# State-space period of a hybrid decoder layer laid out anew: x turned by VectorE, decays a group ahead, taps spread, norm factor on GpSimd

## The reference, cut to what matters

```python
xbc = jax.nn.silu(causal_dwconv(xbc, ssm_conv_w, ssm_conv_b))      # 4 taps
xs, bm, cm = jnp.split(xbc, (D_INNER, D_INNER + SSM_GN), axis=-1)
# in ssd_chunked, with chunks of 128 tokens:
x = (xh * dt[..., None])
decay = jnp.exp(jnp.where(causal, a_cum[..., :, None] - a_cum[..., None, :], -jnp.inf))
cb = jnp.einsum('bclgn,bcsgn->bcgls', cc, bc)
y_diag = jnp.einsum('bcgls,bgrcls,bcsgrp->bclgrp', cb, decay, x)
...
y = y + d_skip[:, None] * xh
y = y * jax.nn.silu(z)
y = y * lax.rsqrt(jnp.mean(y * y, axis=-1, keepdims=True) + NORM_EPS)   # per group of 512
```

## Time and profile before

| | us |
|---|---|
| median of 3 runs | 1932.03 (1931.19 to 1932.3) |
| the profiled execution | 1931.42, of which the span in the trace is 1929.7 |
| TensorE busy | 1916.6 (99%) |
| VectorE busy | 1266.2 (66%) |
| ScalarE busy | 1083.3 (56%) |
| GpSimd busy | 38.3 (2%) |

### The profile page before, as it was taken

How to read it: one execution, slowest core, us unless ns; L and a number is a source line. 1 busy time by engine, 2 the same in 40 slices (tenths; PEclk the granted TensorE clock), 3 DMA queues, 4 the chain that set the end, 5 groups by cost and what they waited for, 6 DMA issues and landing times.

```text
span 1929.7 us, 28955 instructions
## 1 busy us (share of the span) xinstructions
PE 1916.6 (99%) x10258; PEld 1629.8 (84%) x10258; DVE 1266.2 (66%) x1534; ACT 1083.3 (56%) x1474; POOL 38.3 (2%) x79
## 2 busy tenths in 40 slices
PE   9999999999999999999999999999999999999998
PEld 7888888888888878888888888888888888888886
DVE  6777788777878874445444555767766667645444
ACT  6467766677657764444344445666666666534443
POOL 1000000000011100000000000000000000000000
PEclk9999999999999999999999999999999999999999
DMA  7666666656654446666666565666666666665554
GB/s 246 188 191 178 197 190 193 189 171 196 205 163 133 130 132 211 194 194 194 194 191 195 175 239 192 194 185 192 187 194 193 186 185 189 189 198 195 192 193 141
DMA packets 294839, 361.53 MB, mean 187 GB/s; under 512 B 13104, under 2 KB 217968, under 8 KB 293360
## 3 DMA queue, kind: packets, MB, share of 16 engines
q1 hardware_dynamic: 294768, 360.59, 61.0%
HBM read 358.38 MB, written 2.16 MB: 187 GB/s over the span
## 4 chain that ended last, share of the span: by engine, by line
PE 99%; issue 0%; DMA 0%; ACT 0%; DVE 0%; SPq 0%; POOLq 0%; POOL 0%; DVEq 0%; ACTq 0%
PE ps L1405 35%; PE ps L1407 18%; PE ps L1390 14%; PE ps L1391 13%; PE ps L1392 13%; PE ps L1598 1%; PE ps L1526 1%; PE ps L1539 1%; PE ps L1550 0%; PE ps L1599 0%; PE ps L1587 0%; PE ps L1442 0%; DMA raw<-w_in 0%; PE ps L1477 0%; PE ps L1732 0%
## 5 line engine op out<-in xcount | busy, mean ns | idle before, releaser
L870 DVE TENSOR_TENSOR lo<-raw,hi 128x1024 fp32r<-128x1024 f32 x656 | 801.3, 1227 | 518.7 <-ACT hi L449 511.7
L1405 PE MATMUL ps<-uHL,hi 128*128 128x512 f32 x2944 | 1035.5, 396 | 0.0
L449 ACT ACTIVATE hi<-raw 128x1024 fp32r<-128x1024 f32 x656 | 687.2, 1055 | 517.1 <-PE ps L1392 386.2
L1407 PE MATMUL ps<-uHL,lo 128*128 128x256 f32 x2944 | 823.9, 280 | 0.0
L1405 PEld LDWEIGHTS ps<-uHL,hi 128*128 128x128 f32 x2944 | 551.7, 187 | 130.7 <-issue 5.5
L1407 PEld LDWEIGHTS ps<-uHL,lo 128*128 128x128 f32 x2944 | 555.9, 189 | 0.0
L1392 PE MATMUL ps<-hi,aL 128*128 128x512 f32 x384 | 149.5, 389 | 0.0
L1392 PE MATMUL ps<-hi,hL 128*128 128x512 f32 x352 | 136.9, 389 | 0.0
L1391 PE MATMUL ps<-lo,hH 128*128 128x512 f32 x352 | 136.9, 389 | 0.0
L1390 PE MATMUL ps<-hi,hH 128*128 128x512 f32 x352 | 136.9, 389 | 0.0
L454 ACT ACTIVATE hb<-ps 128x512 f32<-128x512 f32 x92 | 54.7, 595 | 121.3 <-PE ps L1407 121.3
(11 more groups left out here) (195 smaller groups left out, 1657.2 us busy)
## 6 DMA issues: line engine op xcount, KB each, us to landing
raw<-w_in SPq DMA_DIRECT2D x265, 512.0 KB, 4.3
raw<-w_ffn_in SPq DMA_DIRECT2D x176, 512.0 KB, 3.7
raw<-w_ffn_out SPq DMA_DIRECT2D x88, 512.0 KB, 4.5
raw<-w_ssm_out SPq DMA_DIRECT2D x64, 512.0 KB, 4.4
raw<-w_attn_out SPq DMA_DIRECT2D x32, 512.0 KB, 4.3
raw<-w_o SPq DMA_DIRECT2D x32, 512.0 KB, 4.3
rows_b<-cum_rows SPq DMA_DIRECT2D x8, 1024.0 KB, 6.8
x_tok<-x SPq DMA_DIRECT2D x8, 256.0 KB, 6.0
```

What stands on the lines that cost most here:

```text
L449: act.activation(hi[:, s % SLOTS, :], raw[:, s % SLOTS, :], ACT.Copy).then_inc(hi_ready, 1)
L870: ve.tensor_tensor(lo[:, s % SLOTS, :], raw[:, s % SLOTS, :], hi[:, s % SLOTS, :].bitcast(F32), ALU.subtract).then_inc(lo_ready, 1)
L1405: pe.matmul(ps[:, pair + c, :], w_hi, uHL[:, kk].rearrange("p a n -> p (a n)"), start=kk == 0, stop=False)
L1407: last = pe.matmul(ps[:, pair + c, 0:SEQ], w_lo, uHL[:, kk, 0, :], start=False, stop=kk == k - 1)
```

## The change

What it does, engine by engine:

- **TensorE** no longer transposes x. `b_dot_c` keeps the two B·C products behind unit 2; `y_of` moves from unit 9 to 11, `mean_y` from 16 to unit 0 of the next period, `turn_root` from 0 to 4.
- **VectorE** transposes x itself in `x_turn`: blocks of 32x32, four instructions behind each of the units 3 to 6, each on 32 partitions and 256 elements, from `sv` to `xd`. The product with dt then works in place. The taps stand in units 9 and 10, 13 and 14, 17 to 19. The blocks stand behind 11 and 12, skip 15, gate 16, sum 19 (two additions for one reduction), mean 3, spread 4, scale 8. `scaled` gives way to `halves` alone.
- **GpSimd** multiplies by `rt` in place (`scaled_in`, five times a period), with the root between.
- **ScalarE** has `conv_start` behind 8, 12, 16, `silu_gate` behind 5, squares behind 18. The next group's `drops` stand behind 15, 16, 17, its first Exp behind 19, the second Exp and the crosses behind 0 and 1. The first group's (`first_decays`) are written apart: behind 0, 1 and 6.
- **SyncE** has `row_load` between units 7 and 8, for every group but the first.

The diff, cut to its core:

```diff
@@ sync
                 columns(U_G + 4, d, "in", g * GW + C_X, KD)
+                if g:
+                    sp.wait_ge(rows_used, g)
+                    row_load(g)
                 columns(U_G + 8, d, "in", g * GW + (C_X + W2), KD)
...
             for g in range(1, G):
                 group(g, g * G_UN)
-                sp.wait_ge(rows_used, g)
-                row_load(g)
                 group_end(g, g * G_UN)
@@ gpsimd
-            with po.Fori(0, G) as g:
-                y_root(g)
+            def scaled_in(t, odd, it, q, done):
+                po.wait_ge(pair_free[(A, B)[(5 * odd + q) % 2]], it * 5 + ((5 * odd + q) // 2 + J_G + 1))
+                po.tensor_tensor(t, t, rt[:, None, :].to_broadcast([P, 2, SEQ]), ALU.mult).then_inc(done, 1)
+            def conv_and_z(odd, it):
+                for q in range(3):
+                    scaled_in(cs[:], odd, it, q, cs_ready)
+                scaled_in(szb[:, 0:2, :], odd, it, 3, z_scaled)
...
+            with po.Fori(1, G // 2) as it:
+                for odd in range(2):
+                    scaled_in(szb[:, 2:4, :], 1 - odd, it + (odd - 1), 4, z_scaled)
+                    y_root(it * 2 + (odd - 2))
+                    conv_and_z(odd, it)
@@ scalar
+            def decay_side(k, u):
+                if u == 15:
+                    drops(k, 0, 0)
+                if u == 16:
+                    drops(k, 0, 1)
+                if u == 17:
+                    drops(k, 1, 0)
+                    drops(k, 1, 1)
+                if u == 19:
+                    decays(k, 0)
+            def decay_rest(k, u):
+                if u == 0:
+                    decays(k, 1)
+                    cross_decays(k, 0, 3)
+                if u == 1:
+                    cross_decays(k, 3, HG)
+                    rows_done(k)
+            def first_decays(u):
+                if u < 2:
+                    for half in range(2):
+                        drops(0, u, half, first=True)
+                if u == 6:
+                    for c in range(2):
+                        decays(0, c)
+                    cross_decays(0, 0, HG)
+                    rows_done(0)
@@ vector
+                    if u == 9:
+                        conv_taps(g * 6, bc_tiles, 0, 2)
+                    if u == 10:
+                        conv_taps(g * 6, bc_tiles, 2, 3)
+                    if u == 13:
+                        conv_taps(g * 6 + 2, low_tiles, 0, 2)
+                    if u == 14:
+                        conv_taps(g * 6 + 2, low_tiles, 2, 3)
+                    if u in (17, 18, 19):
+                        conv_taps(g * 6 + 4, high_tiles, u - 17, u - 16)
...
+            def x_turn(k, q):
+                ve.wait_ge(sv_ready, k + 1)
+                src = sv[q * B32:(q + 1) * B32, 0:4, :].rearrange("p i (c n) -> p i c n", c=TT)
+                for j in range(P // B32):
+                    dst = xd[j * B32:(j + 1) * B32, :, :].rearrange("p c (i n) -> p i c n", i=4)
+                    ve.transpose(dst[:, :, :, q * B32:(q + 1) * B32], src[:, :, :, j * B32:(j + 1) * B32])
...
-                ve.tensor_reduce(ysum[:, :, None], ysq[:].rearrange("p i n -> p n i"), op=ALU.add, axis=AX.X) \
-                    .then_inc(y_summed, 1)
+                ve.tensor_tensor(ysq[:, 0:2, :], ysq[:, 0:2, :], ysq[:, 2:4, :], ALU.add)
+                ve.drain()
+                ve.tensor_tensor(ysum[:], ysq[:, 0, :], ysq[:, 1, :], ALU.add).then_inc(y_summed, 1)
...
-            STEPS = dict(inputs=5, low=8, high=9, skip=12, gate=13, sum=17, mean=19)
+            STEPS = dict(turn=(3, 4, 5, 6), cb=7, inputs=7, low=11, high=12, skip=15, gate=16, sum=19, mean=None)
@@ tensor
-                pe.matmul(ps[:, M, 2 * P:3 * P], sv[:, 4, P:SEQ], sv[:, 5, P:SEQ], start=True, stop=True)
-                for c in range(TT):
-                    for i in range(4):
-                        last = pe.transpose(ps[:, M + 1 + c, i * P:(i + 1) * P], sv[:, i, c * P:(c + 1) * P], ident[:])
-                last.then_inc(x_turned, 1)
+                pe.matmul(ps[:, M, 2 * P:3 * P], sv[:, 4, P:SEQ], sv[:, 5, P:SEQ], start=True, stop=True) \
+                    .then_inc(bc_done, 1)
...
-            def ssd_after(k, u, older=True, at=(2, 9, 16)):
+            def ssd_after(k, u, older=True, at=(2, 11, None)):
                 if u == 0 and older:
+                    mean_y(k - 1)
+                if u == 4 and older:
                     turn_root(k - 1)
```

More of the change, by code:

```diff
@@ L61 @@
 W5 = 512
+B32 = 32
 U_KV = 0
@@ L559, in silu_gate, with drops, decays, cross_decays @@
                 act.activation(szb[:], szb[:], ACT.Silu).then_inc(sz_ready, 1)
-            def drops(k, c):
-                if c == 0:
+            def drops(k, c, half, first=False):
+                if c == 0 and half == 0:
                     act.wait_ge(rows_landed, k * 16 + 16)
-                for h in range(HG):
+                    if not first:
+                        act.wait_ge(y_done, k)
+                for h in range(4 * half, 4 * half + 4):
                     act.activation(dec[:, h, 2 * c, :], rows_b[:, h, c, :], ACT.Relu, scale=-1.0,
                                    bias=acol[:, c, ds(k * HG + h, 1)])
[L569 to L575, removed]
+            def decays(k, c):
+                if c == 0:
+                    act.drain()
+                act.activation(dec[:, :, 2 * c, :], dec[:, :, 2 * c, :], ACT.Exp, scale=-1.0)
+            def cross_decays(k, h0, h1):
+                for h in range(h0, h1):
                     last = act.activation(dec[:, h, 1, :], rows_b[:, h, 1, :], ACT.Exp,
                                           bias=acol[:, 2, ds(k * HG + h, 1)])
-                last.then_inc(decay_ready, 1)
+                if h1 == HG:
+                    last.then_inc(decay_ready, 1)
             def rows_done(k):
@@ L655, in _ @@
             group(0, 0, 0, keys_side)
-            group(1, 1, 0, lambda u: ssd_side(0, u))
+            group(1, 1, 0, second_group_side)
             with act.Fori(1, G // 2) as it:
@@ L1041, in att_side, with conv_taps @@
                     att_logits(h, u // 2 - 1)
[L1043 to L1049, removed]
+            def conv_taps(n0, tiles, t0, t1):
+                if t0 == 0:
+                    ve.wait_ge(conv_first, n0 + 2)
+                for tap in range(t0, t1):
                     sh = TAPS - 1 - tap
@@ L1057, in conv_rest, with z_halves @@
                     ve.drain()
-            def gate_scaled_z(g, odd, it, j):
-                scaled(szb[:, 2 * j:2 * j + 2, :], (A, B)[(5 * odd + 3 + j) % 2], g * 5 + (H_G + 4 + j)).then_inc(z_scaled, 1)
+            def z_halves(g, odd, it, j):
+                halves(szb[:, 2 * j:2 * j + 2, :], (A, B)[(5 * odd + 3 + j) % 2], g * 5 + (H_G + 4 + j))
             def group(g, odd, it, body):
+                bc_tiles = (4, g + 32), (5, g + 40)
+                low_tiles = (0, g * 4), (1, g * 4 + 1)
+                high_tiles = (2, g * 4 + 2), (3, g * 4 + 3)
                 for u in range(G_UN):
@@ L1134, in ssd_scale @@
                 last.then_inc(y_kept, 1)
-            STEPS = dict(inputs=5, low=8, high=9, skip=12, gate=13, sum=17, mean=19)
+            STEPS = dict(turn=(3, 4, 5, 6), cb=7, inputs=7, low=11, high=12, skip=15, gate=16, sum=19, mean=None)
             def ssd_side(k, u, at=STEPS, older=True):
-                if u == 0 and older:
+                if u == 3 and older:
+                    ssd_mean(k - 1)
+                if u == 4 and older:
                     ssd_spread(k - 1)
-                if u == 3 and older:
+                if u == 8 and older:
                     ssd_scale(k - 1)
+                if u in at["turn"]:
+                    x_turn(k, at["turn"].index(u))
+                if u == at["cb"]:
+                    ssd_cb(k)
                 if u == at["inputs"]:
@@ L1166, in _ @@
                     group(g, odd, it, lambda u: ssd_side(g - 1, u))
-            LAST_STEPS = dict(inputs=5, low=7, high=8, skip=11, gate=12, sum=13, mean=15)
+            LAST_STEPS = dict(turn=(3, 4, 5, 6), cb=6, inputs=6, low=7, high=8, skip=11, gate=12, sum=13, mean=15)
             for u in range(X_UN):
@@ L1576, in att_before, with b_dot_c @@
                     turn_probs(h, 2)
-            def turn_x(k, first=False):
+            def b_dot_c(k, first=False):
                 pe.wait_ge(sv_ready, k + 1)
```

62 lines of the change are left out of this document (32 added, 30 removed).

## The result

| | before | after |
|---|---|---|
| median, us | 1931.78 (6 runs) | 1942.12 (6 runs; five of them 1940.68 to 1944.54) |
| the profiled execution, us | 1931.42, span 1929.7 | 1940.68, span 1938.9 |

The ratio is 1.0053, with a 95% interval from 1.0042 to 1.0064: the changed kernel is slower by 10 us. The time lies in the predicted range (1928.5 to 1948), but not at the forecast of 1933.3: of the rivals "VectorE a little over its share" came to pass.

A forecast was written before the change was run, and what follows sets the result against it. TensorE's queue of instructions was taken as the bound (busy 1916.6 of 1929.7 us). The terms -6.3 + 6.1 + 1.5 = +1.3 took 1931.42 to 1932.7, or 1933.3 on the median's scale; range 1928.5 to 1948.

The forecast's parts named there:

- VectorE a little over its share: Rival, chance 0.20: VectorE's transposes of 0.39 to 0.45 us, or small gaps, add 5 to 14 us: 1937 to 1946.
- Part 1: TensorE's queue loses the transposes of x, 0.79 us in each of eight groups: -6.3 us.
- Part 2: SyncE's row load in group 1 delays unit 8's weights; hole in TensorE 5.2 plus 0.9 for VectorE: +6.1 us.
- The 0.9 for VectorE's blocks in group 1: In group 1 VectorE's work before the second half of `y_of` outlasts TensorE's, costing 0.9 us more.
- Part 3: VectorE's load in groups 2 to 7: sixteen transposes at 0.35 us, 5.6 a group; net 0.8 us a group more.
- the upper bound from the rows (0.39): VectorE's transpose would take at most 0.39 us, from an operation with two inputs and a factor of 256 elements.
- Part 4: GpSimd's multiplications at units 10 and 18 meet VectorE's work and cost it 1.1 us each, 2.2 a group.
- The rival of transposes that hold the port: VectorE's transposes hold the port, adding turns of 1.7 us, 12 in all: 1945; shares 0.18 with half-rate transposes.
- Part 5: VectorE's work from `lo` of unit 3 to the second block of decays just fits; 0.2 us a period added: +1.5.
- the break-even of 0.36: VectorE has 5.8 us left for 16 transposes before the second half of `y_of`: 0.36 us each.
- even: Case, chance 0.48: group 1's hole gives back what the transposes brought, -2.8 to +3.6: 1929 to 1936 us.

The follow-up runs named there:

- e7_two_on_ve: The changed kernel with the multiplications by `rt` of units 10 and 14 back on VectorE: 1931.51 us, 0.9998 of the kernel before.
- e8_two_and_late: The changed kernel with units 10 and 14's multiplications on VectorE and group 1's row load behind unit 11's weights: 1926.51 us, 0.9973 of the kernel before.
- e3_half_turns: The changed kernel with eight of VectorE's sixteen transposes a group left out in every group but the first: 1928.29 us, 0.9983 of the kernel before.
- e2_pe_turns: The changed kernel with x transposed by TensorE again, behind the two B·C products: 1935.95 us, 1.0022 of the kernel before.
- e4_ve_scales: The changed kernel with all five multiplications by `rt` a period on VectorE again: 1935.33 us, 1.0017 of the kernel before.
- e5_short: The changed kernel with GpSimd's multiplications of units 10 and 18 cut to 2 columns of 256: 1935.44 us, 1.0020 of the kernel before.
- e9_thirteen: The changed kernel with VectorE doing 13 of the 16 transposes from the second x on: 1932.50 us, 1.0002 of the kernel before.

## Why the prediction was right or wrong

By the experiments the 10.1 us (sure to about 1) between 1932.0 and 1942.1 are made up of three parts. SyncE's queue in group 1, with the clock, is +5.0 (e7_two_on_ve against e8_two_and_late). The ring, with stage X, is +13.8 (changed against e3_half_turns), and the division of e7_two_on_ve takes 10.6 of it away. The gain is -8.7: e3_half_turns is 3.7 below the kernel before and still has the 5.0. The three close to 10.1 by construction, since they are differences of the same medians; the sizes are what they tell. The forecast had +6.1, +1.5 and -6.3.

- **Part 1, the transposes leave TensorE: right, and a little too small.** The period of TensorE's own work falls from 61.04 to 60.17, 0.87 for the 0.79 predicted, and the medians of e2_pe_turns and e3_half_turns are 7.7 apart, for 6.3. A further 1.0 is gained by the new order without them (e2_pe_turns less its hole against before), where the prediction had nothing: before, TensorE's periods were 61.04 to 61.62 without a wait, in e2_pe_turns all 61.04. Why is open.
- **Part 2, SyncE's queue: right in mechanism and nearly in size.** Row load forecast for 116.1, issued 115.90; weights 116.8, issued 116.28; landing 6.9 later, in truth 6.0; hole 5.2, in truth 0.48 + 3.30. The 0.9 for VectorE's blocks in group 1 did not come: none of the five waits for `dec` lies there. What these took less, the clock took more: 1.65 us that the prediction doesn't name. That they nearly cancel (5.0 to 5.5 for 6.1) is luck.
- **Part 3, VectorE's load: the step that failed first.** The duration of a transpose was well bounded (0.436 us; 0.43 was forecast), but the distance of the starts was taken as 0.35, with the overlap of 0.09 that the operations of the earlier trace rows show. Transposes overlap neither each other nor the next `lo`: 0.448, which is over the upper bound from the rows (0.39). 16 x 0.098 = 1.6 us a period, most of what VectorE's part has (31.78) over the 29.8 of the forecast (24.2 + 5.6). The Trainium skill's figure ("VectorE: DVE Perf Modes", The three transpose paths), scaled by the fixed part, had given 0.46 long and 0.37 apart: near in the duration, wrong by the same assumed overlap in the distance.
- **Part 4, GpSimd's turns: right in price, wrong in what they cost.** Two multiplications a period meet VectorE's operations, and each costs it 1.1 (2.85 for 1.75; a pair of taps 1.91 for 0.87), at units 10 and 18 as forecast. At unit 14 GpSimd is the one that waits, 2.21 for 1.29, and VectorE's `lo` at 267.67 loses nothing; the prediction called that one hidden. It is not: ScalarE waits for it. The Trainium skill ("SBUF — State Buffer", SBUF: two separate sides) has whoever starts first keep the ports for the whole instruction; the rows agree. At 267.67 and at 317.29 `lo` started first and lost nothing, and GpSimd waited for it; the skip products that follow at 268.81 (one input in PSUM) lost nothing either, and the block that follows at 318.42 (two inputs in SBUF) waited for GpSimd. The rival of transposes that hold the port is out: at unit 6 both go on as if alone.

```profile
303.46 1.80 DVE L1157 STREAM_TRANSPOSE xd<-sv 32x256 f32<-32x256 f32 x4
303.50 1.30 POOL L414 TENSOR_TENSOR cs<-cs,rt 128x512 f32<-128x512 f32 x1 [9.14 <-DVE cs L971]
```

- **Part 5, does it fit: the break-even of 0.36 was near but too high, and the price above it too low.** By the sum of the ring the transposes may last 7.2 - 2.15 = 5.0 us, 0.31 each, before it is longer than 60.17. Thirteen of them, 5.8 us or sixteen times 0.36, already bring the period to 61.0 and cost 4.2 us in all; 8 leave it at 60.17, 16 make it 62.32. The prediction charged the lag once for each period, as if VectorE began each period afresh. But the end of its gapless part is also the start of the next `cs`, and so of ScalarE's next series: a ring, and what it is longer than TensorE's own period is lost in every period. The head of that ring was seen ("its head waits for a `lo` and for GpSimd's 1.3"), but its four parts were not added up. They are 3.23 + 22.00 + 31.78 + 5.31.
- **Not costed at all: stage X**, where the list of steps puts transposes 3 to 6 and all that follows behind one unit; 1.43 us.
- **The rival came within its terms.** "A little over its share" gave 7 x (16 x 0.09 + 0.2) = 11.5 at 0.45 us a transpose, with the other two terms 1943.3; the time of 1942.1 is in its 1937 to 1946. That it comes so close is luck: the ring with stage X cost 13.8 and the gain was 8.7, each over 2 us more than these terms. It had a chance of 0.20 against 0.48 for even. The price of an operation that no row shows decided between the two, and that price was taken from its cheaper neighbours.

What stays open is the timing of the slow clock. Seven of the kernels have the hole at unit 8, idle for 3.05 to 3.50 us, and in all seven the granted clock fell to 0.50, once. In the changed kernel, e2_pe_turns and e4_ve_scales it fell 0.9 to 1.5 us after TensorE had gone on; in e3_half_turns, e5_short, e7_two_on_ve and e9_thirteen it was down already when TensorE went on. It stayed down for 3.4 us in four of them and for 6.8 in e5_short, e7_two_on_ve and e9_thirteen, so that their holes cost some 1 us more in the traces. No edit explains which. In e7_two_on_ve (waits for `lo` of 0.49 and 3.43 us) work goes on at 125.35:

```profile
124.70:125.20 0.50, 0.00 (x0) 0.00 (x0) 0.50 (x1) 0.50 (x2) 0.00 (x0) 0.51 1.10 385
125.20:125.70 0.50, 0.35 (x1) 0.38 (x2) 0.00 (x1) 0.50 (x1) 0.00 (x0) 0.50 1.08 383
125.70:131.00 5.30, 5.30 (x17) 4.46 (x17) 4.90 (x8) 2.64 (x5) 0.00 (x0) 0.50 0.82 233
```

How much of the 5.0 to 5.5 us is clock and how much hole was measured only in the trace, not by a difference of medians.

## What to carry to other kernels

Where two or three engines hand work round, add up the ring: from one step through all hand-overs to the same step of the next period. If that sum is longer than the bounding engine's own period, the difference is paid in every period, and work moved from a busy engine to an idle one helps only where it leaves the ring; a hand-over to a slower engine on the ring costs more than the work that it takes away. When a new kind of operation is placed in a gapless stretch, charge its full duration until a row shows that it overlaps the next. A single queue with a wait in it (SyncE's) is priced in the period where the wait ends latest, and a hole in TensorE also by what the clock does behind it.

## What the runs showed of the hardware

- VectorE's transposes (32x256, float32) take 422 to 444 ns and start 0.448 us apart on average, while its other operations start 0.08 to 0.09 before the tail of the one ahead is over (0.69 long, 0.61 apart).
- Behind an idle stretch of TensorE of 3.05 to 3.50 us, in each of seven kernels, its granted clock fell from 1.00 to 0.50, once 1.4 us before work went on, once 1.5 us after, and stayed there for 3.4 or 6.8 us; pairs of matmuls then took 0.64 us instead of 0.35. With unneeded transposes in the hole it stayed at 1.00.
- A weight load right behind a 1 MB row load landed 6.0 us after its issue, against 4.3 at the earlier trace rows.
- GpSimd's multiplication of 128x512 by a broadcast: 1.29 alone and 1.30 beside VectorE's transposes, 2.2 when VectorE's `lo` (two SBUF inputs) started 0.16 before it. VectorE's next operation with two SBUF inputs then takes about 1.1 longer (2.85 for 1.75), one with an input in PSUM does not.
